# RWKV inverses in two lanes: from lockstep to eight rounds apart

## The reference, cut to what matters

```
def step(s, inp):
    r_t, w_t, k_t, v_t, kk_t, a_t = inp
    sa = jnp.einsum('bhvk,bhk->bhv', s, -kk_t)
    s = s * w_t[:, :, None, :] + sa[..., None] * (kk_t * a_t)[:, :, None, :] + v_t[..., None] * k_t[:, :, None, :]
    return s, (jnp.einsum('bhvk,bhk->bhv', s, r_t) if with_output else None)
s, ys = lax.scan(step, s0, seq, reverse=reverse)
```

## Time and profile before

| | before |
|---|---|
| median of 3 runs | 5053.02 us (5052.44 to 5054.24) |
| profiled execution, its own time | 5058.15 us |
| its span | 5056.1 us |
| TensorE busy | 4614.6 us, 91% |
| VectorE busy | 2087.9 us, 41% |
| ScalarE busy | 1336.7 us, 26% |
| GpSimd busy | 431.0 us, 9% |
| mean granted clock of TensorE | 0.954 |

### The profile page before, as it was taken

The page is one execution under the profiler, slowest core; times in us unless marked ns, Lnnn a source line. Parts: engine busy times, 40 slices in busy tenths (PEclk is TensorE's granted clock), DMA queues, the critical chain, the costliest instruction groups (busy, mean ns, idle before and its releaser), DMA issues.

```text
span 5056.1 us, 85351 instructions
## 1 busy us (share of the span) xinstructions
PE 4614.6 (91%) x36404; PEld 2842.8 (56%) x36404; DVE 2087.9 (41%) x3866; ACT 1336.7 (26%) x2486; POOL 431.0 (9%) x385
## 2 busy tenths in 40 slices
PE   7899899988998898979998898989999998999999
PEld 3566666666555553464443544544788544444787
DVE  3554555463355542130111336463343237463333
ACT  2333333332222211010000124251232123242232
POOL 0121111110222230000000000020000000020000
PEclk9998999998999999989999899999999999999999
DMA  6200000000111014318998211013321211113321
GB/s 228 81 19 5 18 19 17 5 26 13 42 46 38 34 73 179 118 76 351 407 408 362 97 62 61 35 59 140 115 86 50 87 62 61 43 56 139 113 100 50
DMA packets 76818, 503.33 MB, mean 100 GB/s; under 512 B 9480, under 2 KB 10008, under 8 KB 34328
## 3 DMA queue, kind: packets, MB, share of 16 engines
q1 hardware_dynamic: 76440, 497.88, 25.6%
HBM read 472.66 MB, written 25.19 MB: 98 GB/s over the span
## 4 chain that ended last, share of the span: by engine, by line
PE 79%; DVE 8%; issue 6%; DMA 3%; ACT 2%; POOL 1%; SPq 0%; PEldq 0%; PEld 0%; DVEq 0%; ACTq 0%; POOLq 0%
PE ps L224 76%; PE ps L227 3%; DMA upper<-in_ew 2%; DVE upper L243 2%; ACT upper L282 2%; DVE upper L259 1%; DVE upper L235 1%; POOL upper L3394 1%; DVE upper L251 1%; DVE lower L235 1%; DVE lower L243 1%; ACT lower L282 0%; DVE upper L239 0%; DMA upper<-ybd 0%; DVE lower L239 0%
## 5 line engine op out<-in xcount | busy, mean ns | idle before, releaser
L224 PE MATMUL ps<-lower 128*128 128x512 f32 (+12 forms) x7024 | 1935.6, 444 | 66.5 <-issue 22.8
L224 PEld LDWEIGHTS ps<-lower 128*128 128x128 f32 (+3 forms) x7024 | 958.9, 188 | 782.8 <-issue 610.0
L224 PE MATMUL ps<-upper 64*64 64x64 f32 (+7 forms) x15552 | 829.9, 258 | 144.3 <-DVE upper L251 46.4
L282 ACT ACTIVATE upper<-ps 128x512 f32<-128x512 f32 (+5 forms) x967 | 444.9, 491 | 1769.1 <-PE ps L224 1300.8
L224 PEld LDWEIGHTS ps<-upper 64*64 64x64 f32 (+4 forms) x15552 | 596.9, 145 | 449.7 <-issue 223.8
L224 PE MATMUL ps<-lower,upper 64*64 64x64 f32 (+6 forms) x7536 | 725.3, 316 | 50.5 <-DMA lower<-in_ada 20.3
L224 PE MATMUL ps<-rounded 128*128 128x512 f32 x3072 | 712.3, 394 | 7.5 <-DVEq L213 7.5
L224 PEld LDWEIGHTS ps<-rounded 128*128 128x128 f32 x3072 | 579.6, 189 | 139.4 <-issue 8.3
L224 PEld LDWEIGHTS ps<-lower,upper 64*64 64x64 f32 (+3 forms) x7536 | 384.3, 145 | 337.8 <-issue 267.1
L282 ACT ACTIVATE upper<-upper 128x256 f32<-128x256 f32 (+12 forms) x695 | 361.9, 529 | 725.1 <-DVE upper L255 186.8
L224 PE MATMUL ps<-upper,lower 128*128 128x512 f32 (+4 forms) x1584 | 482.1, 474 | 26.2 <-DMA upper<-yad 11.7
(11 more groups left out here) (81 smaller groups left out, 2139.5 us busy)
## 6 DMA issues: line engine op xcount, KB each, us to landing
lower<-in_ew SPq DMA_DIRECT2D x144, 1024.0 KB, 10.6
upper<-in_ew SPq DMA_DIRECT2D x48, 1024.0 KB, 13.6
lower<-in_b0f SPq DMA_DIRECT2D x16, 2048.0 KB, 8.0
lower<-in_b1f SPq DMA_DIRECT2D x16, 2048.0 KB, 7.9
upper<-in_ada SPq DMA_DIRECT2D x18, 1024.0 KB, 5.4
lower<-in_wrkv SPq DMA_DIRECT2D x8, 1728.0 KB, 7.5
lower<-in_b0g SPq DMA_DIRECT2D x8, 1536.0 KB, 6.7
gad<-upper SPq DMA_DIRECT2D x48, 256.0 KB, 2.0
```

What stands on the lines that cost most here:

```text
L224: return self.e.matmul(out, lhsT, rhs, start=start, stop=stop)
L282: self.e.activation(out, in_, func, bias=bias, scale=scale, accum_out=accum).then_inc(line.up(*event), 1)
```

## The change

The three passes at the start of lane 1 go. In their place each lane passes 8 * d rounds when group 0 has become ready, so lane 1 begins eight rounds after lane 0.

```
     def lane(d):
-        for _ in range(3 * d):
-            yield None
         for j in range(8):
             while j not in ready:
+                yield None
+            for _ in range(8 * d if j == 0 else 0):
                 yield None
             for p in range(3):
                 yield ("tri", j, d, p)
```

## The result

The changed kernel takes 5075.65 us (median of 5 runs, 5071.44 to 5083.24) against 5053.02 before (5 runs, 5049.29 to 5060.76): ratio 1.0045, interval 1.0034 to 1.0056, so it is slower by 22.6 us. The prediction, 5058.4 with a range to 5078, held the time, and missed what made it.

The account below looks back on a forecast made before the run. TensorE, holding 79% of the chain that ended last, was taken as the bound. The terms -3.0, -6, +11, -4, -2.5, +9.9 sum to +5.4 on the profiled 5058.15: 5063.6, or 5058.4 in the median; range 5034 to 5078 us.

Parts of the forecast that it names:

- Kind one: Eleven idle times of about 3.55 us between corner and join, behind shifts on VectorE; waits move, -6 us in all.
- Kind two: Idle at the tail steps, ahead of level 4 and products; lane 0's corner and join now fall there, +11 us.
- Small idle times: Short waits in rounds with projections, about 1.4 us a group; half should go, -4 us.
- kind three: Rounds 351 to 430, without projections, where lanes wait for their own copies; five periods at -0.5, -2.5 us.
- Start: Rounds 47 to 54 lose lane 1's work, but lane 0's copies lose their cover: -3.0 us.
- End: Lane 1's last eight rounds run bound by its cycle, then stepper 1 alone: 18.7 us less 8.8, +9.9 us.
- The clock stays up: Faster rival: half of the eleven waits ahead of join broken up, -28 us of clock, 5030 us; chance 0.14.
- The tail steps cost the clock more: Slower rival: lower clock lasts 13.8 us, not 6.9, behind tail steps; +23 us, 5081, or +11, 5069; chance 0.27.
- The offset pays as meant: Faster rival: unlike steps fill each other's waits everywhere, 5034 us; chance 0.15.
- The sign that I had named for being wrong: A steady group's clock at 0.94 or more would show that the prediction misread what the waits hide.

Follow-up runs that it names:

- e_half: Kernel before, lanes in lockstep, with the order stepper 0, lane 0, lane 1, stepper 1 inside a round: 5027.96 us, ratio 0.9945.
- f_sfirst: Kernel before, lanes in lockstep, with both steppers ahead of both lanes in a round's order: 5003.68 us, ratio 0.9905.
- f_s8: The change (lanes eight rounds apart) made upon f_sfirst, with its order of both steppers first: 5089.31 us, ratio 1.0067.
- g_pair8: Changed kernel, but a stepper waits until both lanes have made its product's inverses, so both steppers issue in the same rounds: 5058.92 us, ratio 1.0009.
- e_alt0: Kernel before, lanes in lockstep, with the order lane 0, stepper 0, lane 1, stepper 1 inside a round: 5079.36 us, ratio 1.0059.
- e_hold0: Kernel before, with the projector passing rounds while a lane is between turn_bk and corner: 5060.39 us, ratio 1.0018.

## Why the prediction was right, and where it was wrong

*The bound.* "A change that only reorders can then win in two ways: TensorE idles less, or its clock is granted at the upper level for longer." That is the sentence that failed. There is a third: the time that the same records take at the full clock depends on their neighbours. I costed "all instructions stay" at nothing, and it was +41.0 us, the largest term. Every number for it stood in the trace of before, where a first `level` of a pair takes 0.515 us and the second, ahead of another shape, 0.577.

*Kind one* (-6 us): right in mechanism, and too small. The waits of 3.55 us ahead of `join` are gone, and the picks behind the same shift now hold up `products`, in rounds 118 and 134 and not 117 and 133, for 2.94 and 3.08 us (I had 3.6), so each of the eleven gave about 1 us and not 0.4 to 0.7. On TensorE:

```profile
365.94 2.69 PE L224 MATMUL ps<-upper 64*128 64x256 f32 x16 [2.94 <-DVE upper L259]
...
415.38 1.77 PE L224 MATMUL ps<-upper 64*128 64x256 f32 x16 [3.08 <-DVE upper L259]
```

On VectorE the shift, the five small operations and only then the pick, as the prediction placed them:

```profile
412.47 1.53 DVE L243 SCALAR_TENSOR_TENSOR lower<-ps,lower 128x511 f32<-128x511 f32 x2
414.03 0.94 DVE L235 TENSOR_TENSOR upper<-lower 128x1 f32<-128x1 f32 x5
414.89 0.44 DVE L259 COPY_PREDICATED upper<-lower,ps 128x256 f32<-128x256 uint8 x1
```

*Kind two* (+11 us): placed right, 0.76 us ahead of `join` (I had 0.95) and 1.77 ahead of `level` 1 in round 160 (1.8), but the small ones that I had set around them were smaller, so that rounds 158 to 161 idle 3.3 us and not 3.95.

```profile
483.72 0.68 PE L224 MATMUL ps<-upper 64*64 64x64 f32 x8 [0.76 <-DVE upper L251]
...
488.96 0.34 PE L224 MATMUL ps<-upper 64*64 64x64 f32 x8 [1.77 <-DVE upper L259]
```

*Small idle times and kind three* (-4, -2.5): a steady group, with kinds one and two in it, idles 11.4 us, not 13.1. The four periods without projections, rounds 367 to 430, idle 17.1 us, not 17.9. The idle time has the sign that I gave it, but a period is not shorter: rounds 415 to 430, all at the full clock in both traces, took 31.4 us before and take 32.7 now (I had 31.1), 1.0 us less idle and 2.3 us more in the steps. *Start* (-3.0): at round 55 the changed kernel is 1.7 us ahead, counted from the first `tri` (22.9 against 24.5), right in sign; by round 63 0.6 is left (210.4 and 210.1 us on the two clocks). Rounds 47 to 94 idle 14.0 us, 3.4 more than before: lane 0's copies had no cover.

*End* (+9.9): from round 431 on it is 26.7 us against 16.2, +10.5; to the last `update` 18.8 us (1231.46 less the 5.07 of the last wait, less 1207.60), where I had 18.7.

```profile
1207.60 0.34 PE L224 MATMUL ps<-upper 64*64 64x64 f32 x8 [1.30 <-DVE upper L259]
...
1231.46 1.09 PE L227 MATMUL ps<-lower,upper 128*128 128x128 f32 x4 [5.07 <-DVE upper L235]
```

All steps are in both kernels, so the +5.4 of my sum was a forecast of idle time over the stage. It came to -0.9: the planning of waits was good to 6 us, in part because its terms missed both ways.

*The rivals.* "The clock stays up" came in part: -17.4 us of the -28 that I gave it. A steady group had three falls before, 6.9 us behind the tail steps and 6.9 to 10.2 behind each of the two waits ahead of `join`; after, two of 6.9. (The recorded far end of this rival, -51 "with the idle time itself gone too", is wrongly added up: eleven times 10.2 times 0.47 is 53 us for the clock alone, and the idle time would be 39 more. It named the reserve rightly, though: e_half and f_sfirst took 44.8 and 46.0 us of it.) "The tail steps cost the clock more" fell: behind them it did not fall at all, the stretch from 440 to 500 us, with the waits of 0.76 and 1.77 in it, is at 1.00. "The offset pays as meant" fell too. The sign that I had named for being wrong, a group's clock at 0.94 or more, did show, and pointed the right way, at a gain; but the group stayed at 136.5 us, inside my 136 to 139. In a group two omissions cancelled. Over the stage +41 and -17 were missing, and the 24 us that they leave fell into a part of the range that I had kept for another case, the tail steps. The range held, but not by its reasons.

## What to carry to other kernels

Where TensorE is the bound and works in tiles of several shapes, count the changes of shape in the order of issue before and after a reordering, and price each; here 0.126 us. Read the price from the trace first: the distance from the last record of a burst to the first of the next, with and without a change of shape. Put steps of like shape side by side, and let what the in-order queues must do at once (here `corner`'s copies) stand ahead of long optional work (a shift): the order in which a round asks its generators did both, in one line, and gave 0.95% (f_sfirst) where the offset lost 0.45%. And read busy time against the clock: the same work, the same length and a higher clock mean that something hidden has grown.

## What the hardware showed unexpectedly

A burst that follows one of its own tile shape starts 0.038 us (64x64) or 0.052 us (128x64) after the last record of the other; one of another shape starts after 0.148 or 0.152 us. A step that has lost its neighbour pays 0.16 to 0.17 us in the rows above (`rest` 0.61 alone, 0.44 as second; `solve` 0.39 and 0.23). In four pairs of kernels with 94 to 331 changes between them this was 0.108 to 0.143 us for a change: f_s8 and f_sfirst, the changed kernel and g_pair8 (31.1 / 279 = 0.111), e_alt0 and before, e_half and f_sfirst. Pairs with fewer changes stray (e_half and before 0.226 for 66; e_hold0, with 16 fewer, +3.3 us), and no run here says what the rest is.

The clock's falls differ in length and not by the wait alone. In the changed kernel, behind waits of about 3 us, it fell to 0.51 for 6.9 us; in f_s8 it fell for 3.4 us behind 3.08 and for 17.1 behind 2.90. Behind 3.55 before it fell for 6.9 to 17.1; behind the 1.56 us at the tail steps of before for 6.9, and behind 1.77 in the changed kernel not at all. What TensorE did ahead of each differs, and no run here settles which part of it decides. In f_s8 and before:

```profile
653.70:657.10 3.40, 3.40 (x60) 3.06 (x61) 2.08 (x5) 0.60 (x1) 2.82 (x4) 0.50 0.03 5
...
701.50:718.60 17.10, 16.10 (x164) 10.22 (x166) 8.33 (x15) 4.80 (x8) 0.52 (x1) 0.50 0.01 2
...
392.10:409.10 17.00, 16.78 (x179) 10.68 (x179) 6.67 (x11) 7.64 (x12) 1.82 (x1) 0.50 0.01 2
```
